# Other section bounds for the FFN layers (4, 6, 6 and 6 inner tiles for 6, 6, 6 and 4) and one more block-product group in each

## What is computed

```python
D_FF = 2816                      # 22 tiles of 128
def swiglu(h, w_in, w_out):
    gate, up = jnp.split(h @ w_in, 2, axis=-1)
    return (jax.nn.silu(gate) * up) @ w_out
xp = xp + 0.5 * swiglu(rms_norm(xp, norm), w_in, w_out)   # the same for xs
```

## Time and profile before

| | us |
|---|---|
| median of 3 runs | 2206.93 |
| lowest and highest run | 2205.39 and 2208.31 |
| profiled execution, its own time | 2210.12 |
| its span, first to last instruction | 2208.4 |
| mean granted TensorE clock, share of full | 0.992 |

### The profile page before, as it was taken

One profiled execution on the slowest core, in us unless ns is written; L12 is line 12 of the kernel. 1 busy time (PEld: TensorE's weight loads), 2 busy tenths in 40 slices (PEclk: granted clock), 3 DMA queues, 4 the chain that ended last, 5 costly groups with the idle time before them and its releaser, 6 DMA issues.

```text
span 2208.4 us, 47374 instructions
## 1 busy us (share of the span) xinstructions
PE 2163.3 (98%) x18666; PEld 2081.2 (94%) x18666; DVE 1583.1 (72%) x2534; ACT 1035.4 (47%) x1861; POOL 171.4 (8%) x243
## 2 busy tenths in 40 slices
PE   9999999999999999999999999999999989999997
PEld 9999999997888999999999999999986679999997
DVE  6888776787436657878768788876557747788875
ACT  6444444552324435444436444444346535444443
POOL 0000002022100010000001000002114511000001
PEclk9999999999999999999999999999999999999999
DMA  4333333233332323333332333333447823333333
GB/s 142 96 114 93 105 101 98 85 103 102 118 125 106 96 87 96 96 106 96 106 101 86 97 95 112 97 100 102 152 149 239 279 79 96 101 92 114 93 102 104
DMA packets 117639, 246.28 MB, mean 112 GB/s; under 512 B 15104, under 2 KB 15376, under 8 KB 116096
## 3 DMA queue, kind: packets, MB, share of 16 engines
q1 hardware_dynamic: 103248, 188.86, 28.2%
q0 software_dynamic: 14048, 54.49, 7.2%
q10 hardware_dynamic: 144, 0.09, 0.0%
HBM read 233.11 MB, written 9.95 MB: 110 GB/s over the span
## 4 chain that ended last, share of the span: by engine, by line
PE 85%; DVE 9%; ACT 3%; issue 2%; DMA 1%; SPq 0%; DVEq 0%; ACTq 0%
PE psum L415 46%; PE psum L460 10%; PE psum L461 10%; PE psum L459 10%; DVE w_low L393 2%; DVE x_low L840 1%; PE psum L2711 1%; PE psum L2726 1%; PE psum L1518 1%; DVE residual L1034 1%; ACT w_high L387 1%; DVE conv_sum L1948 1%; PE psum L2798 1%; DVE probs_by_key L3138 1%; PE psum L2696 1%
## 5 line engine op out<-in xcount | busy, mean ns | idle before, releaser
L393 DVE TENSOR_TENSOR w_low<-w_raw,w_high 128x512 fp32r<-128x512 f32 x703 | 498.4, 719 | 299.1 <-ACT w_high L387 296.5
L387 ACT ACTIVATE w_high<-w_raw 128x512 fp32r<-128x512 f32 x703 | 433.4, 624 | 326.1 <-PE psum L415 226.8
L415 PE MATMUL psum<-x_high,w_high 128*128 128x260 f32 x1664 | 337.1, 284 | 8.3 <-DVE w_low L393 2.8
L415 PE MATMUL psum<-x_low,w_high 128*128 128x260 f32 x1664 | 332.5, 281 | 0.0
L415 PE MATMUL psum<-x_high,w_low 128*128 128x260 f32 x1664 | 332.1, 281 | 0.0
L415 PE MATMUL psum<-hidden_high,w_low 128*128 128x260 f32 x1408 | 282.8, 282 | 0.0
L415 PE MATMUL psum<-hidden_low,w_high 128*128 128x260 f32 x1408 | 282.8, 282 | 0.0
L415 PE MATMUL psum<-hidden_high,w_high 128*128 128x260 f32 x1408 | 282.6, 282 | 0.0
L415 PEld LDWEIGHTS psum<-x_high,w_high 128*128 128x128 f32 x1664 | 256.1, 188 | 15.9 <-DVE x_low L840 4.1
L415 PEld LDWEIGHTS psum<-x_low,w_high 128*128 128x128 f32 x1664 | 256.3, 188 | 0.0
L415 PEld LDWEIGHTS psum<-x_high,w_low 128*128 128x128 f32 x1664 | 255.9, 188 | 0.0
(11 more groups left out here) (440 smaller groups left out, 4364.2 us busy)
## 6 DMA issues: line engine op xcount, KB each, us to landing
w_raw<-in_weights_dram SPq DMA_DIRECT2D x704, 256.0 KB, 2.7
cache_pages<-in_cache_pages_dram POOLq DMA_DIRECT2D x128, 272.0 KB, 4.3
ret_sample_state<-in_state_ret_dram POOLq DMA_DIRECT2D x2, 2048.0 KB, 8.2
out_ret_s_dram<-ret_sample_state POOLq DMA_DIRECT2D x2, 2048.0 KB, 6.6
out_y_dram<-residual SPq DMA_DIRECT2D x8, 260.0 KB, 2.2
ssm_sample_state<-in_state_ssm_dram POOLq DMA_DIRECT2D x2, 1024.0 KB, 5.4
out_ssm_s_dram<-ssm_sample_state POOLq DMA_DIRECT2D x2, 1024.0 KB, 4.8
residual<-in_x_dram SPq DMA_DIRECT2D x3, 520.0 KB, 7.0
```

Source lines behind the costliest of these rows:

```text
L387: nc.scalar.activation(WH[:, slot, :], WRAW[:, slot, :], ACT.Copy).then_inc(w_high, 1)
L393: nc.vector.tensor_tensor(WL[:, slot, :], WRAW[:, slot, :], WH[:, slot, :].bitcast(F32), ALU.subtract).then_inc(w_split, 1)
L415: mm = nc.tensor.matmul(PS[:, b0 + 2 * m + half, 0:cols], w, x[:, half * cols:(half + 1) * cols], start=start, stop=stop)
```

## The change

Sections of 4, 6, 6 and 6 tiles; group 5 becomes a block-product group; the same pattern of a section is used three times, and the former tail of single input steps is gone. The counts of `splits` follow the number of chunks of the next step.

```diff
-SECTIONS = ((0, 6), (6, 12), (12, 18), (18, 22))
+SECTIONS = ((0, 4), (4, 10), (10, 16), (16, 22))
-PLAIN_GROUPS = (0, 1, 2, 3, 5)
+PLAIN_GROUPS = (0, 1, 2, 3)
...
-    order = inner(0, 1, 2, 3, 4, 5)
-    for s in (0, 1):
+    order = inner(0, 1, 2, 3)
+    for s in (0, 1, 2):
         a = SECTIONS[s + 1][0]
         order += inner(a) + out(s, 0) + inner(a + 1, a + 2) + out(s, 1) + inner(a + 3) + out(s, 2)
         order += inner(a + 4, a + 5) + out(s, 3)
-    for g in range(4):
-        order += inner(18 + g) + out(2, g)
...
 (during_s on ACT)
-                splits(3)
+                splits(plan.count[nxt])
...
-                splits(3 if kind(nxt) == "P" else 2)
+                splits(plan.count[nxt] - 1)
...
 (during_s on DVE, both branches; gate(cur) follows)
-                splits(1)
+                splits(plan.count[nxt] - 2)
...
-            if kind(nxt) == "P":
-                up_first(cur)
-                splits(1)
...
 (the last four output steps, ACT and DVE)
-                splits(1)
+                splits(2)
```

## The result

The changed kernel takes 2219.3 us (median of 5 runs, 2217.1 to 2222.1); the kernel before took 2208.3 on the same chip (5 runs). The ratio is 1.005 with a 95% interval of 1.0039 to 1.0061: 8.6 to 13.5 us slower. The forecast was 7.1 us slower, with a range of 2203.5 to 2223 us; on the forecast's base of 2206.9 us the measured difference of 11 us gives 2217.9. The profiled executions took 2219.2 (span 2217.2) and 2210.1 (span 2208.4).

A forecast was written before the change was run, and what follows sets the result against it. PE, busy in 98% of the span, was taken to bound the kernel. Terms -6.2 -2.3 -0.35 +14 +1.6 were given as +7.1 us, on 2206.9 making 2214.0; range 2203.5 to 2223 us.

The forecast's parts named there:

- the last residual: End of b1: with longer output steps the last residual starts at once, 0.35 us less.
- part 1: Sixth group becomes an S group: in each of four FFNs a step of 11.52 us becomes 9.98, 6.2 us less.
- part 2: Two-chunk output steps among S steps: free on PE, but DVE and ACT run late; stalls of 12 to 14 plus 1.6 us.
- ACT's copy: Single S steps behind two-chunk output steps: PE's third product waits 0.2 us for the first product's copy, eight times, 1.6 us.
- part 4: Tail of single S steps becomes pairs behind three-chunk output steps: zero, up to 1 us if loads are late.
- part 3: Three-chunk output steps ending each FFN: x_low waits of 2.3 us at three borders go; bounds 0 to 2.7 us less.
- pair stall: First S step of pairs behind two-chunk output steps: PE's seventh product waits for up_second, 1.5 to 1.75 us, eight times.
- rival B: Third and fourth chunk loads issued close together land later: stalls 1.7 us longer, 2228; in full 0.07 shared with the clock rival.
- rival A: Lateness is absorbed and PE does not stand: only gains stay, -8.9 us, 2198.0; chance 0.10 in full, 0.12 in half.
- cover of 0.4 us: S step behind a three-chunk output step: up_second ends 0.4 us before PE's seventh product is due.
- Rival C: Granted clock falls to half behind each of eight stalls, 1.7 us each, 2228; in full 0.07 shared with rival B.

The follow-up runs named there:

- all three edits: Changed kernel with no pair behind a short output step, up_second behind sums123, and ACT's first-product copy ahead of the fourth chunk's split in single S steps: 0.9951, 2197.8 us.

## Why the prediction was right

The direction, the mechanism and its places held, and the time lay in the range; the loss was under-sized, 7.1 us for 11. The prediction's sum is also added up wrongly: its terms give 6.75 us, and 7.1 leaves out the 0.35 of the last residual (with the stalls at 12 us they give 4.75, not 5.4). This changes nothing in the range or the chances. Term by term, by the traces:

| term | forecast us | in the trace us |
|---|---|---|
| part 1, four steps of 11.52 become 9.98 | -6.2 | -6.1 (FFNs without stalls: 306.45 for 308.0) |
| part 2, eight pairs behind two-chunk steps | +12 to 14 | +16.0 (1.8 to 2.5 each) |
| part 2, eight single steps, ACT's copy | +1.6 | +2.2 (0.23, once 0.58) |
| part 4, pairs behind three-chunk steps | 0 to +1 | +2.5 (3.5 for 1.0) |
| part 3, three borders and the last residual | -2.7 | about -4 (3 x 1.1 and 0.7) |
| sum | +7.1 (its terms: +6.75) | +10.6 |

**The pair stall** was 2.0 us on average and not 1.75. Two things were missing. I took 0.04 us for the restart, and it takes 0.15: the first interval behind it is 0.23 us for 0.12. And the loads' idle time at these eight rows is 2.04 us on average for 1.92 before, some 0.1 more. This is not shown to be rival B (loads close together): the 16 rows behind three-chunk steps in the same trace have 2.15 on average, and the eight rows have 1.94 in the kernel with `up_second` moved. Rival B in full, 1.7 us more at each, did not happen. That the stall goes when the load leaves the chain, and shrinks when `up_second` moves up, shows the mechanism; rival A (absorbed by DVE's idle time) is refuted, since DVE is idle for as long in total and PE stands all the same.

**Part 4 failed as a zero.** The pattern is the old one, but its cover of 0.4 us is used up by any late load, and loads vary between executions. In the changed kernel's trace one of these 16 rows has 3.73 us of idle time, and that pair lost 1.73 us; another has 2.81 and lost 0.81; before, the largest was 2.33.

```profile
168.53 0.69 DVE L947 TENSOR_TENSOR w_sums<-w_raw 128x512 f32<-128x512 f32 x1 [3.73 <-DMA w_raw<-in_weights_dram]
```

I had bounded this by the rows of one execution. Why that load took so long is open; no run was made for it.

**Part 3** brought a little more than forecast. From the end of b0 to the first S step of a1 PE took 47.63 us before and 46.53 after, 1.1 less where the wait for x_low was 0.8; the other two borders became about 1.0 shorter. The mixers differ by up to 5.7 us between executions of kernels that do the same there. The stretch of latent attention took 349.6 to 352.0 us in the five traces in which its mean granted clock was 1.00, and 353.5 to 355.4 in the six in which it was 0.99. So of the 5.7 us that the profiled execution saved outside the FFNs only these 4 are put down to the change.

**Rival C (the clock)** did not happen in the changed kernel's profiled execution, whose FFNs have a granted clock of 1.00 in every window. It happened in the experiment with the sections of 6, 6, 4 and 6, behind stalls of 2.29 and 2.81 us. So the rival was rightly kept, but the prediction's argument against it rests on a wrong reading. It says that the idle time of 2.02 us in attention left the clock at full. The window that starts 0.4 us behind that row's start shows the opposite: the clock was at half (first line). In the changed kernel the same wait, 2.03 us, was indeed followed by full clock (the other two):

```profile
1775.50:1778.50 3.00, 3.00 (x46) 0.50 0.02 5
...
1782.56 1.07 PE L2673 MATMUL psum<-cache_pages,sample_probs_by_key 128*32 128x256 f32 x16 [2.03 <-DVE probs_by_key L3133]
...
1783.00:1786.00 3.00, 3.00 (x70) 1.00 0.04 11
```

An idle time of 2.0 us can thus go either way, and the changed kernel's longest stall in an FFN was 1.77 us. That it stayed clear of the clock was in part luck: by my estimate from these rows, a load half a microsecond later would have brought it to 2.27 us, the size of a stall that was followed by half clock.

**Part 1** came as worked out from the rows. The Trainium skill (TensorE: Matmul & The Clock Gate, section Back-to-back issue gap) would have made part 1 worth 5.3 us at 111 ns a matmul; the gap-free FFNs show 6.1. The same section says that its formula is for a matmul by itself and counts too little for small matmuls in a stream in which each has its own weight load. This stream is one, with as many weight loads as matmuls, and the trace agrees with that: 119 ns at 260 columns where the formula has 111.

## What to carry to other kernels

Shortening a step on the bound engine takes cover away from the in-order queues beside it: walk each queue from the step's start to the one result for which the bound engine waits next, and compare in absolute times, since the busy share (72% before and after) shows nothing of it. In such a queue put the piece that the bound engine waits for ahead of those that it needs later, and place short steps where the next block has idle time; here both together (all three edits) turned a loss of 0.5% into a gain of 0.5%. Size a cover by the latest load that a trace shows with some to spare, and after each removed stall look for the one that stood in its shadow.

## What the runs showed of the hardware

A restart of PE behind a semaphore costs 0.15 us here (the changed kernel's restart at 82.14), not 0.04: 0.05 from the end of the DVE instruction to the first matmul, and 0.11 in a longer first interval.

In the FFNs, stalls between stretches of full work of up to 1.77 us left the granted clock at 1.00 in the changed kernel. Stalls of 2.29 and 2.81 us in the experiment with the sections of 6, 6, 4 and 6 were followed by granted clocks of 0.57 and 0.50 in windows of 2 us, and the pairs around them lost 4.3 and 4.9 us, where its other pairs behind two-chunk steps lost 1.6 to 2.0. In attention an idle time of 2.02 us was followed by 0.50 in the kernel before, and one of 2.03 us at the same place by 1.00 in the changed kernel.

Loads of 256 KB, at a mean of 98 to 100 GB/s, left DVE idle for 1.7 to 3.7 us at the 16 rows of the same kind in one execution of the changed kernel, and for 1.6 to 2.3 us in one of the kernel before. So a chain with a load in it has a spread of up to 2 us.
